# All column pairs with ScalarE's shifts, two scatter units between halves, and stores of one, two, two and three chunks

## The reference

```
a1, a2, b1, b2 = jnp.split(x32, 4, axis=-1)
rot = jnp.concatenate([-a2, a1, -b2, b1], axis=-1)
return (x32 * cos + rot * sin).astype(x.dtype)
```

## Time and profile before

| | us |
|---|---|
| three runs | 1900.81, 1901.68, 1900.98 (median 1900.98) |
| the profiled execution | 1900.78 |
| its span, first to last instruction | 1899.0 |
| TensorE busy | 1777.8 (94%) |
| VectorE busy | 651.9 |
| ScalarE busy | 376.9 |
| GpSimd busy | 330.0 |

### The profile page before, as it was taken

One profiled execution on the slowest core, in us unless ns is written; L12 is line 12 of the kernel. 1 busy time (PEld: TensorE's weight loads), 2 busy tenths in 40 slices (PEclk: granted clock), 3 DMA queues, 4 the chain that ended last, 5 costly groups with the idle time before them and its releaser, 6 DMA issues.

```text
span 1899.0 us, 22343 instructions
## 1 busy us (share of the span) xinstructions
PE 1777.8 (94%) x9262; PEld 1053.6 (55%) x9262; DVE 651.9 (34%) x1328; ACT 376.9 (20%) x853; POOL 330.0 (17%) x193
## 2 busy tenths in 40 slices
PE   6999999999999988788799999999999998888887
PEld 3595567999634333233266755689995343333323
DVE  2853354565411211111158433435643111121103
ACT  3223334101301010010132242340112110101002
POOL 2520006953100000000035100276610000000000
PEclk9999999999999999999999999999999999999999
DMA  9525152425999999999992244214378999999996
GB/s 386 202 92 223 66 221 80 178 89 211 363 419 427 428 427 428 428 428 428 405 392 100 89 183 177 100 45 177 134 293 342 428 428 428 427 428 426 428 429 269
DMA packets 55717, 553.19 MB, mean 291 GB/s; under 512 B 6080, under 2 KB 10560, under 8 KB 13632
## 3 DMA queue, kind: packets, MB, share of 16 engines
q1 hardware_dynamic: 51840, 549.13, 70.0%
q10 hardware_dynamic: 3776, 2.62, 0.4%
HBM read 547.54 MB, written 4.19 MB: 291 GB/s over the span
## 4 chain that ended last, share of the span: by engine, by line
PE 67%; DMA 30%; DVE 2%; issue 1%; SPq 0%; ACT 0%; DVEq 0%
PE psum L1403 17%; PE psum L1644 14%; DMA ring<-in_w_up 9%; DMA dense<-in_w_down 8%; PE psum L1152 8%; DMA ring<-in_w_gate 8%; PE psum L1154 7%; DMA dense<-in_w_gate 4%; PE psum L1161 4%; PE psum L471 2%; PE psum L1322 2%; PE psum L1111 2%; PE psum L1242 1%; PE psum L1606 1%; PE psum L1498 1%; DMA ring<-in_w_in 1%
## 5 line engine op out<-in xcount | busy, mean ns | idle before, releaser
L1644 PE MATMUL psum<-ring,dense 128*64 128x512 f32 x992 | 223.5, 595 | 34.0 <-DMA ring<-in_w_gate 19.0
L1644 PE MATMUL psum<-dense 128*64 128x512 f32 x704 | 159.2, 596 | 22.6 <-DMA dense<-in_w_gate 16.8
L1644 PEld LDWEIGHTS psum<-ring,dense 128*64 128x64 f32 x992 | 71.0, 137 | 177.3 <-issue 144.5
L1152 PE MATMUL psum<-hT,ring 128*128 128x384 f32 x464 | 153.4, 488 | 0.0
L2513 DVE TENSOR_TENSOR state<-state,psum 128x512 f32<-128x512 f32 x32 | 22.0, 689 | 369.7 <-PE psum L1644 331.7
L888 POOL TENSOR_TENSOR tmp<-square 128x384 f32<-128x384 f32 x5 | 5.0, 997 | 817.8 <-ACT square L1780 817.8
L1154 PE MATMUL psum<-ring,hT 128*128 128x512 f32 x288 | 126.5, 594 | 0.0
L1152 PEld LDWEIGHTS psum<-hT,ring 128*128 128x128 f32 x464 | 87.5, 190 | 60.8 <-issue 1.4
L1644 PEld LDWEIGHTS psum<-dense 128*64 128x64 f32 x704 | 50.5, 137 | 125.6 <-issue 92.2
L2088 ACT ACTIVATE kcT<-psum 32x512 f32<-32x512 f32 x60 | 35.2, 587 | 421.0 <-PE psum L1644 420.6
L2550 DVE COPY decays<-psum 16x512 f32<-16x512 f32 x60 | 41.3, 689 | 218.1 <-PE psum L1644 217.7
(11 more groups left out here) (329 smaller groups left out, 2725.1 us busy)
## 6 DMA issues: line engine op xcount, KB each, us to landing
ring<-in_w_in SPq DMA_DIRECT2D x60, 1024.0 KB, 10.4
dense<-in_w_gate SPq DMA_DIRECT2D x30, 2048.0 KB, 36.8
ring<-in_w_up SPq DMA_DIRECT2D x30, 2048.0 KB, 37.4
ring<-in_w_gate SPq DMA_DIRECT2D x30, 2048.0 KB, 36.4
wide<-in_w_up SPq DMA_DIRECT2D x22, 2048.0 KB, 37.9
dense<-in_w_down SPq DMA_DIRECT2D x20, 2048.0 KB, 40.3
ring<-in_w_mod SPq DMA_DIRECT2D x38, 1024.0 KB, 8.6
ring<-in_w_down SPq DMA_DIRECT2D x18, 2048.0 KB, 39.3
```

The source lines that it names most:

```text
L1152: last = M.matmul(psum[:, bank, 0:T], ring[:, n % RING, k, cols], hT[:, k, :], start=k == 0, stop=k == KD - 1)
L1644: last = M.matmul(psum[HALF * half:HALF * (half + 1), bank, :], lhsT(k), SPARE_BLOCKS[2 * kk + half] if spare else w[:, kk, half * SLAB:(h ...
```

## The change

- Slabs 1 (AK) and 6 (CQ, CK) are done in pairs too: eight pairs, two of them (slab 1) ahead of attention between groups 8 and 9, six in the twelve first steps of A. The order of slabs, fillers and of A's and B's steps follows; some groups in B are split in two halves (begun, rest), groups 20 to 21 move from A to B, and B's last two steps have no filler.
- Rope: ScalarE copies the swapped quarters (halves_swapped, four copies of 32 partitions per chunk), VectorE multiplies all 128 partitions by sin, then by cos, and adds. AK's chunks are rotated after the sums of their pair.
- decays() moves ahead of all rotations on VectorE, decay_logs() ahead of the first read on ScalarE.
- The window is added in eight operations of 512 columns, and CK is scaled by ScalarE in B.
- finish_mods(4, 9) and the scale of the second norm move from ahead of the retention heads to m == 2.
- Two of the last scatter's chunks run between the halves of the last down product's second slab, with their residual sums.
- y is multiplied and stored in pieces of 1, 2, 2 and 3 chunks.

The diff, cut to its core:

```diff
+Y_PARTS = [slice(0, 1), slice(1, 3), slice(3, 5), slice(5, KD)]
+SCATTERED_BETWEEN = 2
-FIRST_PAIRED, LAST_PAIRED = 3, 4
-Z_PAIRS = [(slab, p) for slab in (FIRST_PAIRED, LAST_PAIRED) for p in range(2)]
+PAIRED = {1: 12, 3: 4, 4: 16, 6: 20}
+Z_PAIRS = [(slab, p) for slab in PAIRED for p in range(2)]
+PAIRS_AHEAD = 2
...
-        Z_FIRST = 11
+        Z_AHEAD = [0, 1, 2, 3, 8, 9, 10]
...
-                    for g in range(Z_FIRST):
+                    for g in Z_AHEAD[0:5]:
+                        z_group(layer, g)
+                    for i in range(PAIRS_AHEAD):
+                        z_pair(layer, i)
+                        z_half(layer, i)
+                    for g in Z_AHEAD[5:]:
                         z_group(layer, g)
...
                             for k in range(KD):
+                                if k == KD // 2 and part:
+                                    scatter(QUADS - 1, range(SCATTERED_BETWEEN))
                                 if k == KD // 2:
                                     pe.wait_ge(last_rest[part], at(last_rest[part], 16))
...
-                    scatter(QUADS - 1)
+                    scatter(QUADS - 1, range(SCATTERED_BETWEEN, KD))
...
+                    def halves_swapped(c):
+
+                        if c < 4:
+                            sc.wait_ge(z_read, f_of("z", layer, c) + 1)
+                        else:
+                            sc.wait_ge(z_pair_summed, at(z_pair_summed, 4 * (c // 2 - 1)))
+                        if c >= 2:
+                            sc.wait_ge(rope_done, at(rope_done, c - 1))
+                        for q in range(4):
+                            quadrant, other = slice(32 * q, 32 * q + 32), slice(32 * (q ^ 1), 32 * (q ^ 1) + 32)
+                            A_.activation(tmp[other, c % 2, 0:2 * P], zT[quadrant, ROTATED[c], LAT], ACT.Copy).then_inc(rope_part, 1)
+
+                    decay_logs()
+                    for g in Z_AHEAD[0:4]:
                         read_z(layer, g)
-                        if g == 4:
-                            decay_logs()
-                        if g == 5:
-                            decay_inside()
-                        if g == 6:
-                            decay_across()
+                        halves_swapped(g)
+                    decay_inside()
+                    read_z(layer, Z_AHEAD[4])
+                    copy_z_first(layer, 0)
+                    decay_across()
+                    halves_swapped(4)
+                    halves_swapped(5)
+                    copy_z_first(layer, 1)
+                    halves_swapped(6)
+                    halves_swapped(7)
+                    for g in Z_AHEAD[5:]:
+                        read_z(layer, g)
...
-                        for q in range(4):
-                            quadrant, other = slice(32 * q, 32 * q + 32), slice(32 * (q ^ 1), 32 * (q ^ 1) + 32)
-                            V.tensor_tensor(tmp[other, c % 2, 0:2 * P], zT[quadrant, ROTATED[c], LAT], c_("sin")[quadrant], ALU.mult).then_inc(rope_part, 1)
+                    def rotate(c):
+
                         dve.wait_ge(rope_part, at(rope_part, 4 * c + 4))
+                        V.tensor_tensor(tmp[:, c % 2, 0:2 * P], tmp[:, c % 2, 0:2 * P], c_("sin"), ALU.mult)
                         then(V.tensor_tensor(zT[:, ROTATED[c], LAT], zT[:, ROTATED[c], LAT], c_("cos"), ALU.mult))
...
+                    decays()
+                    for c in range(4):
+                        rotate(c)
+                    for i in range(PAIRS_AHEAD):
+                        z_begin_sums(i)
+                        z_end_sums(i)
+                        dve.wait_ge(z_pair_summed, at(z_pair_summed, 4 * i + 4))
+                        rotate(4 + 2 * i)
+                        rotate(5 + 2 * i)
...
-                    finish_mods(layer, 4, 9)
-                    finish_scale(layer, scale_ffn_all, slice(32, 40), slice(56, 64)).then_inc(mod2_ready, 1)
-                    dve.wait_ge(mod2_ready, at(mod2_ready, 1))
...
+                        if m == 2:
+                            finish_mods(layer, 4, 9)
+                            finish_scale(layer, scale_ffn_all, slice(32, 40), slice(56, 64)).then_inc(mod2_ready, 1)
+                            dve.wait_ge(mod2_ready, at(mod2_ready, 1))
...
-                for n in range(KD // 2):
-                    if 2 * n + 2 > KD - len(GAIN_BY_ACT):
-                        dve.wait_ge(y_act, 2 * n + 2 - KD + len(GAIN_BY_ACT))
-                    pair = hT[:, 2 * n:2 * n + 2, :]
+                for chunks in Y_PARTS:
+                    if chunks.stop > KD - len(GAIN_BY_ACT):
+                        dve.wait_ge(y_act, chunks.stop - KD + len(GAIN_BY_ACT))
+                    part = hT[:, chunks, :]
```

More of the change, by code:

```diff
@@ L291, in z_pair_banks @@
         def z_pair_banks(i):
-            a, b, c = [Z_PAIR_BANKS[(i + n) % 3] for n in range(3)]
+            banks = S + TR[1:] if i < PAIRS_AHEAD else Z_PAIR_BANKS
+            a, b, c = [banks[(i + n) % 3] for n in range(3)]
             return a, b, c, a
@@ L526, in build @@
         CHAIN_FILL = [chain_fill(l) for l in range(DEPTH)]
-        FILL = [x for l in range(DEPTH) for x in START_FILL[l] + [("z", l, g) for g in range(Z_FIRST)]
-                + [y for step in A_FILL[l] + B_FILL[l] for y in step if y[0] not in ("pair", "half")] + CHAIN_FILL[l]]
+        FILL = [x for l in range(DEPTH) for x in START_FILL[l] + [("z", l, g) for g in Z_AHEAD]
+                + [("z",) + y[1:] if y[0] == "rest" else y for step in A_FILL[l] + B_FILL[l] for y in step if y[0] not in ("pair", "half", "begun")] + CHAIN_FILL[l]]
         def f_of(kind, l, i):
@@ L1140, in z_group @@
                             first_half_here(n)
-                        if g == 19:
-                            pe.wait_ge(z_pair_summed, at(z_pair_summed, 4 * len(Z_PAIRS)))
                         bank = bank_free(f)
                         cols = slice(j * P, (j + 1) * P)
-                        begun = g < BEGUN[l]
-                        for k in range(KD // 2 if begun else 0, KD):
+                        if g < BEGUN[l]:
+                            chunks = range(KD // 2, KD)
+                        for k in chunks:
                             if j == 0 and k == KD // 2:
@@ L1166, in z_weights @@
                         slab, p = Z_PAIRS[i]
-                        return [[z_weight_quarter(layer, slab, p, kh, nh) for nh in range(2)] for kh in range(2)], Z_WEIGHT_SUMS[p]
+                        return [[z_weight_quarter(layer, slab, p, kh, nh) for nh in range(2)] for kh in range(2)], Z_WEIGHT_SUMS[i]
                     def z_pair(l, i):
@@ L1205, in fill @@
                         for kind, l, i in step:
-                            {"mod": mod_slab, "modT": mod_transposed, "z": z_group, "norm": a_norm, "pair": z_pair, "half": z_half}[kind](l, i)
+                            {"mod": mod_slab, "modT": mod_transposed, "z": z_group, "norm": a_norm, "begun": z_begun, "rest": z_rest, "pair": z_pair, "half": z_half}[kind](l, i)
                     if layer == 0:
@@ L1707, in picks_transposed, with scatter @@
                         last.then_inc(pgT_full, 1)
-                    def scatter(quad):
+                    def scatter(quad, chunks=range(KD)):
                         pe.wait_ge(down_act, at(down_act, QUAD * (quad + 1)))
@@ L1715, in scatter @@
                             pe.wait_ge(xg_dve, at(xg_dve, 2 * (quad + 2)))
-                        for n in range(KD):
+                        for n in chunks:
                             if quad == QUADS - 1 and n == 4:
@@ L1856, in read @@
                         for kind, l, i in step:
-                            {"mod": read_mod, "modT": read_modT, "z": read_z, "norm": read_norm, "pair": copy_z_first, "half": none_to_read}[kind](l, i)
+                            {"mod": read_mod, "modT": read_modT, "z": read_z, "norm": read_norm, "begun": none_to_read, "rest": read_z, "pair": copy_z_first, "half": none_to_read}[kind](l, i)
                     if layer == 0:
@@ L2513, in gated, with residual @@
                         V.tensor_tensor(hid, act, psum[:, S[1], :], ALU.mult).then_inc(hid_ready, 1)
-                    def residual(quad):
-                        for n in range(KD):
+                    def residual(quad, chunks=range(KD)):
+                        for n in chunks:
                             dve.wait_ge(sc_full, at(sc_full, KD * quad + n + 1))
```

116 lines of the change are left out of this document (70 added, 46 removed).

## The result

| | runs | median, us | lowest to highest |
|---|---|---|---|
| before | 20 | 1901.38 | 1900.21 to 1903.52 |
| after | 20 | 1904.66 | 1900.26 to 1908.95 |

The ratio is 1.002 (95% interval 1.0014 to 1.0026): slower by 3.3 us, where 1898.0 was forecast. The times of after are spread over 8.7 us, those of before over 3.3, and they go with the granted clock of the whole run: the two runs at 0.999 took 1900.26 and 1901.19, the six at 0.997 1902.5 to 1904.8, the four at 0.992 to 0.994 1908.7 to 1908.9. The profiled execution of after is one of the slower ones, 3.2 above its median: 1907.89, span 1906.0, clock 0.995, against 1900.78, 1899.0 and 0.999.

What follows compares the result with a forecast made beforehand. TensorE's dense work and the tail after the last slab were taken as the bound. Terms -9.8 - 0.8 + 8.1 + 1.5 + 0.7 - 1.5 - 1.2 + 0 = -3.0 from 1900.98 gave 1898.0 us, range 1889 to 1903.

Steps and rivals of the forecast that it cites:

- (a): Dense stretch: four more column pairs per layer, each saving 1.22 us; 4.88 per layer, 9.8 us less for both.
- (b): Before the first scores: TensorE's rope waits of 0.56 and 0.68 go, pair 2 waits about 0.2 each; net -0.8 us.
- rope rival: Layer 0: VectorE's rotations, at 2.0 us per operation beside GpSimd's sums, become the bound; +11, 1909; chance 0.12.
- (c): Start of both layers: TensorE waits before group 2 for a read held behind decay_logs(); 4.0 and 4.1, together +8.1 us.
- (d): TensorE's clock falling to half at the two waits of 4 us; one fall taken, +1.5 us.
- two-fall case: TensorE's clock falls at both of the 4 us waits before group 2: 3.0 us, or more if it stays low.
- (e): B steps: first norm's wait grows from 0.27 to 0.6, +0.7 us for both layers; other moved pieces cost nothing.
- (f): finish_mods moved behind head 2: TensorE's wait of 0.73 for the decayed scores goes, -1.5 us for both layers.
- (g): Two scatter units between the last product's halves: worth 1.32, last half 0.7 late; -0.6 per layer, -1.2 us.
- (h): Final stores of y in pieces of 1, 2, 2, 3 chunks: between -0.4 and +0.5 us, taken as 0.
- The sign that I had set: Forecast wrong if the dense stretch, first group to first expert product, is over 4 us shorter or any longer than before.
- the long low clock: Rival: both waits at group 2 lose the clock, for twice as long; 6.0 us instead of 1.5, 1902.5; chance 0.15.

Runs made afterwards that it cites:

- the run with both moves: Kernel after with decay_logs() behind group 1's shifts and, in layer 0's step 7 of B, group 29 between the two modT; 1892.27 us, ratio 0.9953.
- the run with the token sums held back: Kernel after with GpSimd's four token sums waiting for abs_ready, behind the first half of decays, logarithms still ahead of the first read; 1898.8 us, ratio 0.9987.
- the run with late logarithms: Kernel after with decay_logs() on ScalarE behind the reads and shifts of groups 0 and 1; 1897.59 us, ratio 0.9981.
- the run with one scatter unit: On top of the run with both moves: one scatter unit instead of two between the halves, store pieces of 2, 2, 2, 2 chunks; 1894.1 us, ratio 0.9955.

## Why the prediction was wrong, step by step

- **(a) Pairs.** Right: 112 records of two pairs take 18.20, 9.10 each. In the run with both moves TensorE is busy for 486.59 in layer 1's dense stretch, against 491.44 in before: 4.85 less for the 4.88 of the forecast.
- **(b) Rope's wait.** Right that it goes; ScalarE's read then holds pair 2 for 0.46, where I had 0.2. The rope rival fell: rotations go at 1.37 to 1.49 per operation, under the 1.6 that I gave them, and are done at 91.38. But its mechanism is what makes pair 1 wait 0 to 2.55 by chance in the kernels without the group-2 waits.
- **(c) The wait at group 2.** Right in place, cause and size: 3.46 + 3.67 = 7.1 for 8.1. The read of group 0 is over at 49.31 as forecast (49.2); the wait of layer 0 is shorter because group 1 ended at 45.9, not at 45.30. GpSimd's part in it is shown by the run with the token sums held back. The Trainium skill's page "SBUF — State Buffer", section "Who interferes with whom", has a reduction pass and an operation of two SBUF inputs locked out for a whole GpSimd operation. The trace agrees: 0.29 for the reduction, 1.71 and 1.72 for the two inputs, at 128 and at 8 columns.
- **(d) The clock.** The first step that failed, by its size. I took one fall, +1.5. The profiled execution had one behind each of the three waits, 1.5, 1.5 and 1.8 (12.28 for 32 records against 10.48) = 4.8. A fourth, behind a wait of 2.02 at 1730.88, fell into layer 1's expert stretch. In the median, filling the two group-2 waits with work took off 2.4 by itself. I had written the two-fall case (3.0), and chose the middle with no row for it. Nor were the 2.9 us that I compared my waits with a lower bound: the wait of 2.42 had its fall too.
- **(e) The moved pieces of B.** The step that failed, by its substance: "the modulation products and split groups are the same work in another order" costs nothing only if the order of reads on ScalarE allows it. The work was the same, but modT, modT, z in one step made group 29 wait for a read queued behind exponentials: 2.42, with a fall behind it. I asked there whether softmax would be late, not which read frees which bank. The norm's wait was 0.68 for the 0.6 forecast; two modulation products that wait in each layer, one 0.35 for VectorE's pair sums and one 0.23 for ScalarE's read of a transposition, were missed.
- **(f) finish_mods.** Right: both waits of 0.73 are gone.
- **(g) Scatter units.** -0.39 per layer for -0.6: the last half is 0.9 late (2.46 to 3.38 between halves), not 0.7 (0.1 of it is my reading: by the earlier trace rows the first half ends at 948.84, not at 948.73), and ScalarE's last square waits 0.33 for GpSimd's adds.
- **(h) Stores.** Right within its bounds: 0.1 for the pieces. The other 0.3 by which the end is longer comes with every kernel built on after. It lies behind VectorE's last operation of y (3.41 from there to the end with the pieces of before, against 3.13); why, I don't know.

The sum: forecast -3.0. In the profiled executions the span is 7.0 longer. Of the difference of 10.0, 3.3 is (d), 2.4 the wait of step 7, 0.7 the modulation products that wait for pair sums, 0.5 those that wait for a transposition's read, 0.5 pair 2, 0.1 the norm, 0.4 (g), 0.6 the later start of group 0 in layer 0, 1.4 the expert stretches and 0.3 the end; (c) gives 1.0 back. That makes 9.2; the other 0.8 I haven't traced. The start and the expert stretches differ as much between two executions of like kernels, so they are chance and no step of the prediction. The median missed by 6.7, less than the profiled execution; the 3.2 between them are worth about two falls, an estimate from the 1.5 to 1.8 of each. The sign that I had set came true in both layers: dense stretches longer than before's. Of the rivals the long low clock, 1902.5, came nearest. The chance of 0.12 for slower was too small for a kernel where a wait may cost its length and 1.5 us more.

## What to carry to other kernels

A fixed order of reads that frees banks is a contract between two lists: when fillers are moved, write down for each product which read frees its bank and what that read is queued behind; equal work is no equal cost. Never put a chain of small operations between engines ahead of such a read while GpSimd works on SBUF: here each one but the reduction took as long as a GpSimd operation, 1.2 to 1.8. And price a wait of TensorE of several microseconds at its length plus what a fall of the clock took here (1.5), or fill it with matmuls that end before it does.

## What the runs showed of the hardware

I had thought of the clock as a risk behind waits of 4 us. In the twelve profiled executions all five waits of 3.46 to 3.67 had a half-clock stretch behind them; of the twenty waits of 2.0 to 2.7 twelve had one; no shorter wait had. (The first wait of each execution, for the first slab, is left out.) So two executions of one kernel differ by where it falls. Of two waits of 2.43 at the same place, in step 7 of B, the one was followed by 16 records in 7.09 (the run with late logarithms), the other by 16 in 5.40 (token sums held back):

```profile
238.97 7.09 PE L1184 MATMUL psum<-hT,ring 128*128 128x384 f32 x16 [2.43 <-ACT mod_columns L1861]
```
```profile
240.44 5.40 PE L1185 MATMUL psum<-hT,ring 128*128 128x384 f32 x16 [2.43 <-ACT mod_columns L1862]
```

The kernel before is not free of the longer waits: in most executions one slab or two of an expert stretch come 1 us late, in before's at 1713.92 with a wait of 2.28 and no fall. Eight of the seventeen falls are in expert stretches. TensorE's timeline of the run with one scatter unit:

```profile
736.35 3.65 PE L1685 MATMUL psum<-ring,dense 128*64 128x512 f32 x16 [1.34 <-DMA ring<-in_w_gate]
742.06 5.35 PE L1685 MATMUL psum<-ring,dense 128*64 128x512 f32 x16 [2.05 <-DMA ring<-in_w_gate]
```

There the 1.7 us cost the end almost nothing, since the slabs around it wait some 1 us for their transfers anyway: that expert stretch took 428.49, against 428.68 in before. The five executions with a fall in layer 0's expert stretch took 428.1 to 429.1 for it, the seven without 427.7 to 429.4; in layer 1's it was 428.0 to 428.4 for three and 427.7 to 428.3 for nine. In the dense stretches, where TensorE is the bound, the 1.5 to 1.8 are paid in full. Why a slab is late I didn't look into.
